# The diagonal mask of the forgetting heads on GpSimd, the output weight's pieces spread over the heads, and one output sum a step earlier

## The chip, the cores and the metric

One core of a Trainium2 chip runs the kernel. Five engines work from queues of their own: TensorE (PE; its weight loads are shown as PEld), VectorE (DVE), ScalarE (ACT), GpSimd (POOL) and SyncE (SP), which issues DMA transfers here. They meet at semaphores only. The metric is the time of one execution on the device in microseconds.

## What is computed

One step of a hybrid attention layer: a prompt of 1024 tokens and 8 running streams of 16 tokens, of width 1024. The input is normalised and projected; eight forgetting heads and eight stick-breaking heads of 64 columns attend; the group outputs are normalised, gated, and go through one output projection with a residual sum and a last norm. For the change only the prompt's forgetting heads count:

```python
def fox_attend(q, k, v, cq, ck, q_pos, k_pos):
    s = jnp.einsum("bqhd,bkhd->bhqk", q, k, preferred_element_type=jnp.float32) * (HEAD_DIM ** -0.5)
    bias = jnp.swapaxes(cq, 1, 2)[:, :, :, None] - jnp.swapaxes(ck, 1, 2)[:, :, None, :]
    mask = k_pos[None, :] <= q_pos[:, None]
    p = jax.nn.softmax(jnp.where(mask, s + bias, -jnp.inf), axis=-1)
    return jnp.einsum("bhqk,bkhd->bqhd", p.astype(v.dtype), v)
```

The queries come in 8 tiles of 128 rows. The query's own sum `cq` is constant in a row and falls out of the softmax, so the kernel adds only the key's forget sum to the scores, and masks the upper triangle of the diagonal tile.

## The kernel before, in words

The program has three stages. In the first (to about 655 us) the projection of all tokens runs beside the attention of the running streams. In the second the prompt's 16 heads follow one another, eight forgetting heads (g = 0) and then eight stick-breaking heads (g = 1). The third merges the groups and writes the output. The change is in the second stage.

**Heads and units.** A head `h` has 8 units `u`; unit `u` is query tile `i = 7 - u` and needs `8 - u` tiles of keys, so a head goes from 1024 columns down to 128. `pair` (one function on each engine) goes through the steps of two heads; `run_pairs` calls it, in a loop of the hardware for the middle pairs. Every engine's order is written out by hand, and the engines differ in which unit they hold in a step: in step `u` TensorE and VectorE work ahead on unit `u + 3` (`AHEAD`), ScalarE on unit `u + 2`. So step 5 holds the next head's unit 0, step 6 its unit 1, step 7 its unit 2.

**One unit of a forgetting head.**
- `scores` (lines 1180 to 1203, TensorE): two products for each segment of up to 512 columns, into the pair of banks of `u % 2`, then one bf16 product of `identb` and `mask[g]` that adds the mask on the diagonal tile (L1201). It waits for `s_moved` of unit u-2, which had the same banks.
- `maxima` (L1469 to L1479, VectorE): adds the forget sums `c_b` to the scores into `pr` and takes the row maximum (L1475; its second instruction reads the maximum out), then scales it (L1478). `c_b` is loaded by a DMA for each head (`load_c`), one buffer for each head of a pair, and its next load waits for the last maximum.
- `softmax` (L1373, ScalarE): the exponential with the row's sum.
- `transpose_p` (L1205, TensorE) turns the exponentials in groups of four tiles into two banks; ScalarE (even groups, L1425) and VectorE (odd groups, L1515) copy them out to `pT`.
- `outputs` (L1225, TensorE): products with the values, two units at a time, in the even steps.

**The output of a head** comes in two halves (units 0 to 3, units 4 to 7). ScalarE copies a half out (`move_o`, L1393), TensorE turns it in four transposes into bank `MI` (`turn`, L1250 to L1261), ScalarE copies its odd columns (`move_odd`, L1400), and VectorE takes the reciprocals of the row sums (L1494), adds even and odd columns (L1504) and multiplies by the reciprocals (L1506) (`store_o`, L1487). The first half is turned in step 6 (`TURN_AT`) and summed in step 7; the second half of head h-1 is turned at the end of step 4 of head h (`TURN_LAST_AT`) and copied and summed in step 5:

```python
if u == TURN_LAST_AT + 1:
    if hh:
        store_o(p, 0, 1, g)
    elif later(p, 1):
        store_o(p - 1, 1, 1, int(g and not (isinstance(p, int) and p == NPAIR)))
```

The same bank `MI` also takes the next head's keys (`turn_k_of`, L1162, in steps 1 and 2), which ScalarE rounds (`split_k`, L1370) and VectorE completes with a low part (`prep`, L1466). The turn of the second half waits for that low part (L1254).

**The output weight.** `load_wo` loads it in four parts, `split_wo` (L1615 to L1625, GpSimd) multiplies each by the norm gains in place (four instructions of 128x2048, L1621), ScalarE rounds it in eight pieces (`round_wo`, L1627, one in each step of head 6), and GpSimd writes the low parts in four instructions (L1625). In the forgetting heads GpSimd has nothing else to do. In the stick-breaking heads it has one product for each unit (L1558).

## Time and profile before

| | us |
|---|---|
| median of 3 runs (lowest, highest) | 1067.99 (1067.46, 1069.05) |
| the profiled execution's own time | 1065.78 |
| its span in the trace | 1064.0 |
| TensorE busy, share of the span | 1014.4, 95% |
| VectorE | 664.6, 62% |
| ScalarE | 463.3, 44% |
| GpSimd | 254.9, 24% |
| mean granted clock of TensorE, of full speed | 0.999 |

The profiled execution is one run, here 2.21 us below the median. Between span and time lie 1.8 us outside the first and the last instruction. Busy times overlap: an engine's share says nothing yet of what bounds a stage, and the waits in the timeline do.

### The profile page before, as it was taken

How to read it: one execution, taken by the hardware profiler on the slowest of the kernel's cores; microseconds unless marked ns; L12 is line 12 of the kernel's file. 1: busy time of each engine (PE TensorE's matmuls, PEld its weight loads, DVE VectorE, ACT ScalarE, POOL GpSimd, SP SyncE). 2: the span in 40 equal slices, each digit the busy share in tenths (PEclk: the TensorE clock that was granted, in tenths of full speed). 3: DMA queues.
4: the chain of work that ended last, by engine and by line, in shares of the span. 5: the costliest groups of instructions: out<-in, count | busy, mean ns of one | idle time of the engine just before them, and what ended most of it. 6: DMA issues, size and time to landing. Idle time of an engine off the chain costs nothing.

```text
span 1064.0 us, 27363 instructions
## 1 busy us (share of the span) xinstructions
PE 1014.4 (95%) x11316; PEld 854.3 (80%) x11316; DVE 664.6 (62%) x982; ACT 463.3 (44%) x912; POOL 254.9 (24%) x197
## 2 busy tenths in 40 slices
PE   5899999999999999999999998999988999999997
PEld 5898778986778888988888987777766788787786
DVE  5657455654665446665555723676767877787387
ACT  5522312222131232232222323676687787787453
POOL 2300000000000000111201110400065566565497
PEclk9999999999999999999999999999999999999999
DMA  6367697698889787779888787855444342421343
GB/s 228 110 238 235 226 329 294 252 363 318 305 326 339 296 304 284 301 286 362 305 314 318 278 240 238 221 138 130 112 95 98 93 110 60 99 70 51 139 159 139
DMA packets 121472, 234.02 MB, mean 220 GB/s; under 512 B 60552, under 2 KB 91272, under 8 KB 103952
## 3 DMA queue, kind: packets, MB, share of 16 engines
q1 hardware_dynamic: 96016, 209.33, 58.2%
q10 hardware_dynamic: 25344, 23.08, 6.3%
q8 instruction: 85, 1.39, 0.5%
q14 instruction: 27, 0.22, 0.1%
HBM read 204.52 MB, written 27.86 MB: 218 GB/s over the span
## 4 chain that ended last, share of the span: by engine, by line
PE 79%; DVE 6%; issue 4%; POOL 4%; ACT 4%; DMA 1%; ACTq 1%; DVEq 0%; POOLq 0%; SPq 0%
PE bank L887 29%; PE bank L874 8%; PE bank L951 7%; PE bank L997 6%; PE bank L1245 5%; PE bank L1677 5%; PE bank L1221 5%; PE bank L1198 4%; PE bank L980 3%; DVE pr L1475 2%; PE bank L1260 1%; PE bank L1176 1%; DVE om L1485 1%; POOL o_nat L1850 1%; POOL m_stat L1837 1%
## 5 line engine op out<-in xcount | busy, mean ns | idle before, releaser
L887 PE MATMUL bank<-w_hi,hT_hi 128*128 128x256 f32 (+1 forms) x896 | 261.0, 291 | 3.7 <-DVE hT_lo L620 3.3
L887 PE MATMUL bank<-w_lo,hT_hi 128*128 128x256 f32 (+1 forms) x896 | 253.4, 283 | 0.0
L887 PE MATMUL bank<-w_hi,hT_lo 128*128 128x256 f32 (+1 forms) x896 | 253.0, 282 | 0.0
L887 PEld LDWEIGHTS bank<-w_hi,hT_hi 128*128 128x128 f32 x896 | 170.9, 191 | 11.1 <-issue 5.3
L887 PEld LDWEIGHTS bank<-w_lo,hT_hi 128*128 128x128 f32 x896 | 171.1, 191 | 0.3 <-issue 0.2
L887 PEld LDWEIGHTS bank<-w_hi,hT_lo 128*128 128x128 f32 x896 | 170.7, 191 | 0.0
L534 ACT ACTIVATE u_out<-bank 128x256 f32<-128x256 f32 x112 | 42.9, 383 | 269.5 <-PE bank L887 269.2
L730 DVE STREAM_TRANSPOSE k_buf<-k_buf 128x2048 f32<-128x2048 f32 x64 | 145.3, 2292 | 3.6 <-DMA k_buf<-in_cache_sb_k 3.3
L1485 DVE TENSOR_TENSOR_SCAN om<-om 128x1024 f32<-128x1024 f32 (+3 forms) x64 | 110.4, 1729 | 14.3 <-ACT om L1386 13.6
L1558 POOL TENSOR_TENSOR pr<-pr,om 128x1023 f32<-128x1023 f32 (+3 forms) x64 | 90.4, 1419 | 77.9 <-DVE om L1485 75.1
L1221 PE MATMUL bank<-ident,pr 128*128 128x128 f32 x576 | 85.8, 276 | 8.1 <-ACT pT L1425 3.9
L1198 PE MATMUL bank<-k_hl,q_hh 128*128 128x512 f32 x192 | 76.4, 398 | 9.5 <-DVE rowmax L1475 6.0
L1245 PE MATMUL bank<-pT,v_nat 128*64 128x128 f32 x1152 | 83.6, 278 | 0.0
L747 DVE TENSOR_TENSOR_SCAN d_om<-d_om 128x2064 f32<-128x2064 f32 x8 | 35.7, 4458 | 74.6 <-ACT d_om L565 74.6
L1245 PEld LDWEIGHTS bank<-pT,v_nat 128*64 128x64 f32 x1152 | 68.1, 137 | 10.7 <-issue 10.6
L951 PE MATMUL bank<-k_buf,q_cur 32*32 32x512 f32 x2048 | 73.8, 598 | 0.4 <-issue 0.3
L1515 DVE COPY pT<-bank 128x512 f32<-128x512 f32 (+2 forms) x80 | 38.1, 476 | 55.4 <-PE bank L1221 53.1
L1221 PEld LDWEIGHTS bank<-ident,pr 128*128 128x128 f32 x576 | 61.9, 141 | 12.0 <-POOL pr L1558 3.8
L845 POOL TENSOR_TENSOR d_pn<-d_pn,d_om 128x15 f32<-128x15 f32 x8 | 3.7, 459 | 270.0 <-DVE d_om L747 270.0
L838 POOL CAST pick_cur<-pickf 128x128 fp32r<-128x128 bf16 x8 | 2.3, 293 | 272.4 <-PE bank L964 272.4
L997 PE MATMUL bank<-v_ring,d_pT 128*32 128x128 f32 x2048 | 65.9, 275 | 0.0
L1198 PE MATMUL bank<-k_hl,q_ll 128*128 128x512 f32 x192 | 64.0, 346 | 0.0
(208 smaller groups left out, 1934.2 us busy)
## 6 DMA issues: line engine op xcount, KB each, us to landing
k_buf<-in_cache_fox_k SPq DMA_DIRECT2D x32, 1024.0 KB, 9.1
v_ring<-in_cache_fox_v SPq DMA_DIRECT2D x32, 1024.0 KB, 6.8
k_buf<-in_cache_sb_k SPq DMA_DIRECT2D x32, 1024.0 KB, 8.5
v_ring<-in_cache_sb_v SPq DMA_DIRECT2D x32, 1024.0 KB, 7.1
w_raw<-in_w_in SPq DMA_DIRECT2D x14, 1024.0 KB, 9.9
out<-u_out ACTq DMA_DIRECT2D x72, 128.0 KB, 4.8
q_scratch<-u_out ACTq DMA_DIRECT2D x64, 128.0 KB, 5.3
k_nat<-out SPq DMA_DIRECT2D x32, 256.0 KB, 4.0
```

Of the source, the lines that this page charges most:

```text
L534: act.activation(u_out[:, r % UO, :], bank[:, U + i % 2, 0:NCOL], ACT.Copy).then_inc(u_moved, 1)
L730: dve.transpose(chunk, chunk).then_inc(kx_done, 1)
L874: mm = pe.matmul(bank[:, b, :], a[c % 2][:, k, cols], h[:, k, toks], start=(k == 0 and n == 0), stop=(k == KD - 1 and n == 2))
L887: mm = pe.matmul(bank[:, U + i % 2, w_cols(c)], a[:, k, hcols(s)], b[c % 2][:, k, w_cols(c)], start=(k == 0 and n == 0), stop=(k == KD - 1 ...
L951: mm = pe.matmul(bank[32 * j:32 * j + 32, DSC + r, :], q_t[rows_r, half, h, :], k_buf[rows_r, :, at:at + 32], start=(g == 1 and hh == 0 an ...
L997: mm = pe.matmul(bank[2 * DS * j:2 * DS * j + 2 * DS, MIX, 0:P], d_pT[:, 4 * c + t, 2 * DS * j:2 * DS * j + 2 * DS], v_ring[:, q % NV, t, ...
L1198: mm = pe.matmul(out, a[:, hh, i * P:i * P + P], k_hl[:, hh, seg * 512:seg * 512 + w], start=(a is q_hh), stop=(a is q_ll and not diagonal ...
L1221: mm = pe.transpose(bank[:, turn_at(u, lr, g), (j % 4) * P:(j % 4) * P + P], pr[:, u % 4, j * P:j * P + P], ident[:])
L1245: mm = pe.matmul(bank[part, PV, (i % 4) * P:(i % 4) * P + P], v_nat[:, j, hh * HD:hh * HD + HD], turned_p(hh, lr)[:, (j % 4) * P:(j % 4) * ...
L1485: dve.tensor_tensor_scan(x, x, x, 1.0, ALU.mult, ALU.bypass).then_inc(scan_done, 1)
L1558: pool.tensor_tensor(x, x, om[:, u % 4, 1:n], ALU.mult).then_inc(pb_ready, 1)
L1677: mm = pe.matmul(out, a[:, k, :], b[:, first + k, cols], start=(k == 0 and n == 0), stop=(k == NPAIR - 1 and n == 2))
```

## The change

Three things are done in the forgetting heads; the stick-breaking heads keep their order and their mask products.
- The mask product goes for g = 0. In its place GpSimd writes the masked value into the forget sums `c_b` themselves, on the 128x128 tile of unit u's diagonal (`hide_ahead`), before VectorE adds them. Earlier units of the head still need that tile unmasked, so the mask of unit u waits for `s_moved` of unit u-1 (unit 0 for the load alone), and the maximum of unit u waits for the mask (`c_hidden`).
- The pieces of the output weight become 16 multiplications and 16 low parts of 128x512. They are issued one by one behind the masks: the multiplications one in each unit of heads 1 and 2, the low parts one or two in each unit from head 6, unit 4 on.
- The second half of the last head's output is turned in step 4 before the step's transposes (before: after its outputs), its odd columns are copied in step 4 behind ScalarE's exponential, and VectorE sums it in step 4 behind the maximum, in place of step 5.

```diff
@@ scores
-                    diagonal = seg == i // 4
+                    diagonal = seg == i // 4 and g
...
-                        mm = pe.matmul(out[:, w - P:w], identb[:], mask[g][:], start=False, stop=True,
+                        mm = pe.matmul(out[:, w - P:w], identb[:], mask[1][:], start=False, stop=True,
@@ pair of TensorE
+                    if not g and u == TURN_LAST_AT and later(h, 1):
+                        turn(h - 1, 1)
                     transpose_p(p, hh, u, g)
...
-                    if u == TURN_LAST_AT and later(h, 1):
+                    if g and u == TURN_LAST_AT:
                         turn(h - 1, 1, last=following is None)
@@ pair of ScalarE
-                    if u == TURN_LAST_AT + 1 and later(h, 1):
+                    if g and u == TURN_LAST_AT + 1:
                         move_odd(h - 1, 1)
...
                         softmax(*ahead_of(p, hh, u, AHEAD - 1))
+                    if not g and u == TURN_LAST_AT and later(h, 1):
+                        move_odd(h - 1, 1)
@@ maxima
                 wait_unit_free(dve, p, hh, u)
+                dve.wait_ge(c_hidden, k + 1)
                 plain_wait(dve, sc_ready, k + 1)
@@ pair of VectorE (store_last holds the old four lines)
-                    if u == TURN_LAST_AT + 1:
+                    if g and u == TURN_LAST_AT + 1:
+                        store_last(p, hh, g)
...
                     if ahead:
                         (scans if g_ahead else maxima)(*ahead)
+                    if not g and u == TURN_LAST_AT:
+                        store_last(p, hh, g)
@@ pool_prompt
-            split_wo(pool)
+            for h in range(NHEAD // 2):
+                for u in range(NU):
+                    hide_ahead(pool, h, u)
+                    j = NU * h + u
+                    if 0 <= j - SPLIT_AT < 2 * KD:
+                        scale_wo(pool, j - SPLIT_AT)
+                    if j >= LOWS_AT:
+                        for n in range(3 * (j - LOWS_AT) // 2, min(3 * (j - LOWS_AT + 1) // 2, 2 * KD)):
+                            lower_wo(pool, n)
...
+        SPLIT_AT, LOWS_AT = NU, NU * (NHEAD // 2 - 2) + 4
+
+        def hide_ahead(pool, h, u):
+            hh, i = h % 2, TP - 1 - u
+            if u == 0:
+                pool.wait_ge(cb_loaded[hh], 16 * (h // 2 + 1))
+            else:
+                pool.wait_ge(s_moved, NU * h + u)
+            x = c_b[:, hh, i * P:i * P + P]
+            pool.affine_select(out=x, in_=x, compare_op=ALU.is_ge, fill=MASKED, base=0,
+                               pattern=[[-1, P]], channel_multiplier=1).then_inc(c_hidden, 1)
+
+        def wo_piece(ap, j):
+            return ap[:, j // 2, W * (j % 2):W * (j % 2) + W]
+
+        def scale_wo(pool, j):
+            if j == 0:
+                pool.wait_ge(gn_loaded, 32)
+            if j % 4 == 0:
+                pool.wait_ge(wr_loaded[j // 4], 16)
+            gain = gn_col[:, j // 2:j // 2 + 1].to_broadcast([P, W])
+            pool.tensor_tensor(wo_piece(wo_raw, j), wo_piece(wo_raw, j), gain, ALU.mult).then_inc(wog_done, 1)
+
+        def lower_wo(pool, j):
+            pool.wait_ge(wohi_done, j // 2 + 1)
+            pool.tensor_tensor(wo_piece(wo_lo, j), wo_piece(wo_raw, j), wo_piece(wo_hi, j).bitcast(F32), ALU.subtract
+                               ).then_inc(wolo_done, 1)
```

`round_wo` now waits for two of the smaller multiplications, and the first users of the low parts for 8 and 16 of them.

## Rows read from the trace of the kernel before

**Rows 1.** Busy time by stretch, one head each; columns in the first line.

```profile
core 0: us, PE busy (x) PEld busy (x) DVE busy (x) ACT busy (x) POOL busy (x), PEclk, DMA share, GB/s
...
709.42:727.49 18.07, 17.02 (x163) 13.73 (x159) 13.15 (x39) 12.23 (x28) 0.00 (x0) 1.00 0.49 118
...
764.45:784.64 20.19, 17.59 (x164) 13.89 (x159) 13.73 (x39) 17.27 (x34) 9.35 (x3) 1.00 0.62 138
```

**Rows 2.** Waits of TensorE, 658 to 800 us: total, times, longest.

```profile
PE bank L1198 <- DVE rowmax L1475: 6.0, 15, 0.9
```

**Rows 3.** Timeline of TensorE in head 2, steps 5 to 1: start, length, instruction.

```profile
706.04 0.48 PE L1198 MATMUL bank<-k_hl,q_hh 128*128 128x512 f32 x1
...
707.05 0.23 PE L1201 MATMUL bank<-mask_fox,identb 128*128 128x128 bf16 x1
...
707.12 0.50 PE L1221 MATMUL bank<-ident,pr 128*128 128x128 f32 x3
...
709.68 0.66 PE L1260 MATMUL bank<-ident,oT 128*128 128x128 f32 x4
...
710.71 0.50 PE L1198 MATMUL bank<-k_hl,q_hh 128*128 128x512 f32 x1 [0.36 <-DVE rowmax L1475]
...
714.57 0.19 PEld L1198 LDWEIGHTS bank<-k_hl,q_hh 128*128 128x128 f32 x1 [0.32 <-DVE rowmax L1475]
```

**Rows 4.** Timeline of head 0, steps 5 to 7, VectorE and TensorE.

```profile
672.28 0.56 DVE L1515 COPY pT<-bank 128x384 f32<-128x384 f32 x1 [2.37 <-PE bank L1221]
...
672.76 1.22 DVE L1475 CUSTOM_DVE_ANT_0 pr<-bank,c_b 128x1024 f32<-128x1024 f32 x1
...
674.31 0.66 PE L1260 MATMUL bank<-ident,oT 128*128 128x128 f32 x4
...
674.72 0.48 PE L1198 MATMUL bank<-k_hl,q_hh 128*128 128x512 f32 x1
```

**Rows 5.** Timeline of VectorE in head 2, steps 5 to 0.

```profile
707.75 0.56 DVE L1515 COPY pT<-bank 128x384 f32<-128x384 f32 x1 [2.81 <-PE bank L1221]
...
709.03 0.42 DVE L1506 TENSOR_TENSOR o_nat<-o_nat,rowinv 128x256 f32 x1
709.42 1.23 DVE L1475 CUSTOM_DVE_ANT_0 pr<-bank,c_b 128x1024 f32<-128x1024 f32 x1
...
710.89 1.09 DVE L1475 CUSTOM_DVE_ANT_0 pr<-bank,c_b 128x896 f32<-128x896 f32 x1
...
712.21 0.29 DVE L1515 COPY pT<-bank 128x128 f32<-128x128 f32 x1
...
713.56 0.95 DVE L1475 CUSTOM_DVE_ANT_0 pr<-bank,c_b 128x768 f32<-128x768 f32 x1
...
715.35 0.81 DVE L1475 CUSTOM_DVE_ANT_0 pr<-bank,c_b 128x640 f32<-128x640 f32 x1
```

**Rows 6.** Timeline of GpSimd at the start of the span.

```profile
1.23 0.29 POOL L2057 TENSOR_SCALAR_AFFINE_SELECT ident<-ident 128x128 f32<-128x128 f32 x1 [0.25 <-POOL neghalf L2055]
```

**Rows 7.** Timeline of TensorE in head 1, scores of units 0 and 4.

```profile
688.37 0.48 PE L1198 MATMUL bank<-k_hl,q_hh 128*128 128x512 f32 x1
...
696.44 0.50 PE L1198 MATMUL bank<-k_hl,q_hh 128*128 128x512 f32 x1
```

**Rows 8.** Timeline of head 3, steps 2 to 4.

```profile
719.48 0.66 PE L1176 MATMUL bank<-ident,k_nat 128*128 128x128 f32 x4
...
720.80 0.69 DVE L1466 TENSOR_TENSOR k_hl<-bank,k_hl 64x512 fp32r<-64x512 f32 x1 [0.61 <-ACT k_hl L1370]
...
721.66 0.66 PE L1221 MATMUL bank<-ident,pr 128*128 128x128 f32 x4 [0.41 <-ACT pT L1425]
```

**Rows 9.** Timeline of GpSimd and VectorE in head 0; the low parts, grouped by form.

```profile
663.35 14.28 POOL L1621 TENSOR_TENSOR wo_raw<-wo_raw,gn_col 128x2048 f32<-128x2048 f32 x4 [34.79 <-DMA wo_raw<-in_w_out]
...
676.76 1.15 DVE L1506 TENSOR_TENSOR o_nat<-o_nat,rowinv 128x256 f32<-128x256 f32 x1
...
L1625 POOL TENSOR_TENSOR wo_lo<-wo_raw,wo_hi 128x2048 fp32r<-128x2048 f32 x4 | 18.5, 4627 | 99.2 <-ACT wo_hi L1629 99.2
```

**Rows 10.** Timeline of ScalarE at the end of head 7.

```profile
800.40 0.38 ACT L1400 ACTIVATE o_odd<-bank 128x256 f32<-128x256 f32 x1 [0.96 <-PE bank L1260]
```

More of the change, by code:

```diff
@@ L1506, in store_o, with store_last @@
                     dve.tensor_tensor(dst, dst, inv, ALU.mult).then_inc(on_done, 1)
+            def store_last(p, hh, g):
+                if hh:
+                    store_o(p, 0, 1, g)
+                elif later(p, 1):
+                    store_o(p - 1, 1, 1, int(g and not (isinstance(p, int) and p == NPAIR)))
             def pair(p, g, g_next):
@@ L1515, in pair @@
                             dve.tensor_copy(*move_pt(dve, p, hh, u, n, g)).then_inc(pt_moved_dve, 1)
-                    if u == TURN_LAST_AT + 1:
-                        if hh:
-                            store_o(p, 0, 1, g)
-                        elif later(p, 1):
-                            store_o(p - 1, 1, 1, int(g and not (isinstance(p, int) and p == NPAIR)))
+                    if g and u == TURN_LAST_AT + 1:
+                        store_last(p, hh, g)
                     if u == (TURN_AT if g else TURN_AT + 1):
@@ L1613, in load_wo @@
                 sp.dma_start(wo_raw[:, 2 * c:2 * c + 2, :], wo_v[:, 2 * c:2 * c + 2, :]).then_inc(wr_loaded[c], 16)
[L1615 to L1625 removed]
+        SPLIT_AT, LOWS_AT = NU, NU * (NHEAD // 2 - 2) + 4
[21 more added lines that the diff above has]
+                               ).then_inc(wolo_done, 1)
         def round_wo(act, k):
[L1628 removed]
+            act.wait_ge(wog_done, 2 * k + 2)
             act.activation(wo_hi[:, k, :], wo_raw[:, k, :], ACT.Copy).then_inc(wohi_done, 1)
@@ L1684, in a_product @@
                 pe.wait_ge(yalo_done, s + 1)
-                pe.wait_ge(wolo_done, 2)
+                pe.wait_ge(wolo_done, KD)
             else:
```

15 lines of the change are left out of this document (2 added, 13 removed).

## The prediction

> **What bounds the kernel now.** I read the page first: TensorE is busy 95% of the span, and the lines of the change all run in one stage, the eight forgetting heads, from about 655 to 801 us. So I cut that stage at each head's first maximum. A plain head takes 18.07 us, of which TensorE is busy 17.02, VectorE 13.15 and ScalarE 12.23, with GpSimd idle [rows 1]. Head 6 takes 20.19 with ScalarE busy 17.27 (it rounds the output weight there) [rows 1]. TensorE is the bound of the head, but not everywhere: in the waits of TensorE over the stage the largest named one is the scores that wait for VectorE's maxima, 6.0 us in 15 waits [rows 2]. Then I read where in a head this wait lies, from the timeline of head 2.
>
> TensorE scores three units ahead, into two pairs of banks, so the scores of unit u wait until VectorE has reduced unit u-2. In step 5 it starts unit 0 of the next head at 706.04, turns the head's first output half at 709.68, and starts unit 2 only at 710.71, 1.03 us later [rows 3]. In head 0, where step 5 has no sum of an earlier head, the same pair stands 0.41 us apart (674.31, 674.72) [rows 4]. So 0.62 us of a head are lost there, and the timeline of VectorE says why: its copy of step 5 starts at 707.75, and the maximum of unit 0 only at 709.42 [rows 5], 1.67 us later, because reciprocal, sum and product of the previous head's second half stand between; in head 0 the maximum stands at 672.76, directly behind the copy. Everything behind is shifted too: the maximum of unit 1 at 710.89, the copy of step 7 at 712.21 [rows 5], and the scores of unit 4 at 714.57 [rows 3].
>
> **The moved sum, first stretch (unit 0 to unit 4 of the next head).** Before it takes 714.57 - 706.04 = 8.53 us [rows 3]. After the change I rebuild it from VectorE's rows. The copy starts at 707.75 less the one mask product in front of it, 707.69. From copy to maximum head 0 has 672.76 - 672.28 = 0.48 us [rows 4], so unit 0's maximum starts at 708.17 and ends 1.23 later, at 709.40. Before, the next maximum starts 710.89 - 709.42 - 1.23 = 0.24 us behind it [rows 5]. Now a GpSimd instruction lies between: the end of unit 0 releases the mask of unit 1, which releases VectorE.
>
> That round trip is shown by no row of before. The instruction itself is: an affine select of 128x128 f32 takes 0.29 us, and it started 0.25 us after the GpSimd result that it waited for [rows 6]. The lower bound is 0.29 (hand-overs free), the upper 0.25 + 0.29 + 0.25 = 0.79 (that wait on both sides). I take 0.5, since VectorE starts 0.24 us after its own result with a small instruction in between, so its own side of the hand-over must be short. Unit 1 then starts at 709.9 and ends 1.09 later, at 711.0, and the copy of step 7 starts 0.23 behind that as before, at 711.25. From that copy to unit 4's scores is 714.57 - 712.21 = 2.36 us (copy, reciprocal, sum, product, maximum of unit 2) [rows 3, 5]. The scores of unit 4 start at 713.61, 7.57 us behind 706.04: **0.96 us less**. TensorE alone would need 8.53 less the waits of 0.62 and 0.32 in it [rows 3], 7.59 with four masks or 7.33 without them, so VectorE's chain stays the bound by a little, and only one of the four removed masks counts here; the other three are worth nothing, covered by that chain. Heads 2 to 5 get this, 3.8 us. In head 1 the stretch was only 696.44 - 688.37 = 8.07 us [rows 7], so 0.5. In head 6 ScalarE is nearly full; between nothing and 1.5 I take 0.9, as its stretch is the same code with more to wait for. Sum 5.2 us.
>
> **The sum in step 4.** It isn't free of cost on TensorE: the four turns now stand in front of the step's transposes, and they wait for the second half of the next head's keys. Before, these are turned at 719.48, their low part is written at 720.80 to 721.49, the step's transposes start at 721.66 after waiting 0.41 us for ScalarE, and the turns come last, behind the outputs [rows 8]. After: the turns at about 721.6, the transposes 0.41 later at 722.05, where they no longer wait, the outputs behind them, and the next head's scores at 724.1 where they were before. So neither gain nor loss, except that the masks of units 6 and 7 lie in front of a wait and give nothing. ScalarE copies the odd columns behind its transposed copy and exponential of that step, at an estimated 724.2, so VectorE's sum and product end at about 725.4. The copy of step 5 follows the next scores by 707.75 - 706.04 = 1.71 us, so at 725.8, and before it VectorE idled 2.81 us [rows 3, 5]: that idle time hides the sum. If it ends later than 725.8, the old stall comes back by as much; the room is about 0.4 us.
>
> **The mask product.** What follows it starts 0.07 us after it (707.05, 707.12) [rows 3], and in front of it no gap is left that it alone would make. So it costs about 0.065 us; 64 would be 4.2 us. On the path are those of units 4 and 5 in the second stretch, and a 0.05 us rest: 0.18 us in each of 7 heads, 1.3 us. By the Trainium skill (TensorE: Matmul & The Clock Gate, Back-to-back issue gap) a stream of 128-column products goes at about 81 ns each; by that figure the 64 would be worth 5.2 us, and the sum would be 0.3 us larger.
>
> **The weight's pieces.** Before, GpSimd scales in four instructions from 663.35 on, 14.28 us, and VectorE's product of two SBUF inputs that started at 676.76 took 1.15 us: it ended at 677.91, 0.28 us after GpSimd's 677.63 [rows 9]; in head 2 it takes 0.42 [rows 5]. That hold of 0.7 us stands in front of unit 2's maximum and goes, as head 0 has no pieces any more: 0.75 us with a mask. A scaling piece is a sixteenth, 0.9 us, in heads 1 and 2; a lower piece is a quarter of 4.63, 1.16 us [rows 9], in heads 6 and 7, at most two in a step of 2.3 us. A mask behind a piece waits for it, but a piece starts just behind a mask, beside the maximum that this mask released. I found one late place, unit 4 of head 7 by about 0.9 us, whose scores have over 2 us of room. What such pieces can still hold is the product in step 7 of heads 1, 2 and 6: 0.1 us each, 0.3 in all, a loss.
>
> **The rest.** The first head starts cold: masks of units 1 and 2 wait on the maxima before, 2 x (0.5 - 0.24) = 0.5 us lost, TensorE waiting. At the end of head 7 ScalarE's copy of 0.38 us at 800.40 [rows 10] leaves the path to the first sigmoid: 0.4 us won. No DMA is moved; the forget sums of the next pair are loaded after the last maximum, as before.
>
> **Sum:** 5.2 + 1.3 + 0.75 + 0.4 - 0.5 - 0.3 = 6.85 us. The profiled execution took 1065.78 us (span 1064.0 and 1.8 around it), so 1058.9 for it; it was 2.2 below the median of 1067.99. Against that median, by which it will be measured: **1061.1 us**. About 2.1 us (0.2%) is what can be told from no change.
>
> **Rivals.** *A smaller gain.* The hand-over takes 0.79 and the moved turns push step 4's transposes: 6 stretches and the start's two masks lose 0.29 each (2.3 us), the rest of the second stretch 0.2 in 7 heads (1.4). Left: about 3.1, 1064.9 us. For it: every step of the new chain is serial. Against: the masks are outside the loop except at unit 1. *No change:* TensorE's turns in step 4 wait long for the keys' low part and VectorE's sum ends well behind 725.8, so the stall of step 5 stays; only hold and masks are won: 1 us, 1067.0. Against it the 2.81 us of idle time; for it that the turns' wait ends only 0.1 us ahead of where they are wanted. *Slower:* the round trip over GpSimd. Its place is between two maxima; units 0 to 1 have 0.24 us before, units 2 to 3 have 715.35 - 713.56 - 0.95 = 0.84 [rows 5]. If the trip takes 1.5 us, the first stretch loses 1.0 more, which is its gain, and unit 5's scores come 0.6 later in 7 heads (4.2), and the start loses 2.5: with what is won elsewhere some 5 us over, 1073. It decides from a trip of about 1.2 us. Such a trip needs GpSimd held by VectorE. The maximum of 1024 columns at 672.76 ran while GpSimd scaled, and took 1.22 us, as in head 2 without GpSimd (1.23) [rows 4, 5, 9], so GpSimd doesn't hold the maximum, and a maximum that isn't held is unlikely to hold GpSimd; only the product of two SBUF inputs is held. The Trainium skill (GPSIMD Engine Reference, Specifications) says that GpSimd's SBUF interfaces are shared with VectorE, with contention for VectorE instructions of two SBUF inputs or in a two-port mode; the traces agree for the first, and the maximum has one input in PSUM. *More:* the masks count everywhere and head 6 gives 1.5: 10 us, 1058.
>
> **Chances.** Forecast 0.52, smaller gain 0.20, no change 0.14, slower 0.10, more 0.04. Faster by over 0.2%: 0.76; within: 0.14; slower: 0.10. The range goes from 1057.5 (the largest case) to 1066.5, which takes in the bound 0.79 and leaves out the slower case and half of no change.
>
> **What would show it.** Plain heads of about 17.0 us; turn to unit 2's scores 0.41 us apart; maximum of unit 0 0.5 us behind the copy of step 5; maximum of unit 1 about 0.5 us behind the end of unit 0's; affine selects of 0.29 us; copies of wide tiles unchanged; the product of two SBUF inputs never over 1.5 us. It is wrong if affine selects take over 0.6 us, if VectorE idles for GpSimd in more than two units of a head, or if the sum of step 4 reaches past the copy of step 5.

## The result, and the profile after

The changed kernel took 1062.02 us (median of 4 runs, 1060.02 to 1063.22), the kernel before beside it 1068.52 (4 runs, 1067.46 to 1069.33): ratio 0.9942, 95% interval 0.9919 to 0.9965. It is faster, by 6.5 us. Two more measurements of the unchanged file are below: their medians lie 4.0 and 5.9 us under the kernel before (ratios 0.9959 and 0.9953), so this first one is the largest of three.

The profiled execution took 1063.22 us. The page of the changed kernel, first lines and the busy times:

```profile
span 1061.4 us, 27412 instructions
## 1 busy us (share of the span) xinstructions
PE 1013.3 (95%) x11252; PEld 858.1 (81%) x11252; DVE 664.3 (63%) x982; ACT 464.9 (44%) x912; POOL 277.5 (26%) x285
```

That execution is only 2.56 us shorter than the profiled one of before, and the page can't say why. Cut at the heads' first maxima, as for [rows 1], it can be said. The first maximum starts at 660.25 us, in the trace of before at 657.35: 2.9 us were lost ahead of the changed stage. The stage itself, up to the first scan (VectorE's first instruction for the stick-breaking heads), takes 140.50 us in place of 146.67, so 6.17 less; and 0.70 us come back behind it. That is a sum: the first head behind the stage alone is 1.30 us longer (last section). I compare stages from here on, because they repeat: the same kernel gave 140.50, 140.50 and 140.52 us in three traces, while its whole runs scatter by 3 to 8 us.

Busy time by stretch in the changed kernel, heads 0 to 7 and the first head behind the stage; columns as in [rows 1]:

```profile
660.25:675.83 15.58, 13.58 (x120) 11.41 (x119) 10.91 (x32) 10.83 (x24) 3.32 (x9) 1.00 0.98 326
675.83:692.75 16.92, 16.20 (x152) 13.73 (x151) 13.34 (x40) 12.35 (x28) 10.35 (x16) 1.00 0.72 177
692.75:709.94 17.19, 16.41 (x152) 13.81 (x151) 13.40 (x39) 12.36 (x28) 9.37 (x15) 1.00 0.65 151
709.94:727.29 17.35, 16.53 (x154) 13.88 (x152) 13.17 (x39) 12.36 (x28) 2.31 (x8) 1.00 0.53 126
727.29:744.76 17.47, 16.10 (x149) 13.58 (x149) 13.16 (x38) 12.38 (x28) 2.31 (x8) 1.00 0.64 150
744.76:761.88 17.12, 16.30 (x153) 13.80 (x152) 13.17 (x39) 12.35 (x28) 2.31 (x8) 1.00 0.47 121
761.88:780.67 18.79, 16.28 (x151) 13.49 (x150) 13.46 (x38) 16.74 (x34) 10.35 (x15) 1.00 0.66 148
780.67:800.75 20.08, 17.93 (x171) 14.75 (x169) 14.08 (x39) 17.10 (x34) 13.89 (x17) 1.00 0.35 82
800.75:824.36 23.61, 19.96 (x155) 16.21 (x154) 18.84 (x20) 17.82 (x36) 15.63 (x11) 0.86 0.39 82
```

The second number is the length of a head. Row 709.42 of [rows 1] (18.07 us) answers to 709.94 here (17.35), row 764.45 (20.19) to 761.88 (18.79). GpSimd, idle in a plain head before, now has its eight masks there, 2.31 us. Cut so, head 7 became longer, 20.08 from 19.38, and head 0 by 0.17. Where the cut lies matters: before, head 7's first maximum stood 3.84 us behind TensorE's first scores for it (784.64 and 780.80), now 2.03 (780.67 and 778.64). From its first scores to the first scan, head 7 takes 22.11 us in place of 23.22.

How a head was rebuilt is in the timeline of the changed kernel around the start of a head (steps 4 to 7):

```profile
705.36 0.63 PE L1261 MATMUL bank<-ident,oT 128*128 128x128 f32 x4 [0.55 <-DVE k_hl L1471]
705.82 0.60 PE L1222 MATMUL bank<-ident,pr 128*128 128x128 f32 x4
...
707.81 0.50 PE L1199 MATMUL bank<-k_hl,q_hh 128*128 128x512 f32 x1
...
708.16 0.42 DVE L1510 TENSOR_TENSOR o_nat<-bank,o_odd 128x256 f32 x1 [0.76 <-ACT o_odd L1403]
...
708.62 0.42 DVE L1512 TENSOR_TENSOR o_nat<-o_nat,rowinv 128x256 f32 x1
...
709.47 0.56 DVE L1527 COPY pT<-bank 128x384 f32<-128x384 f32 x1 [0.42 <-PE bank L1222]
...
709.94 1.21 DVE L1481 CUSTOM_DVE_ANT_0 pr<-bank,c_b 128x1024 f32<-128x1024 f32 x1
...
711.31 0.29 POOL L1643 TENSOR_SCALAR_AFFINE_SELECT c_b<-c_b 128x128 f32<-128x128 f32 x1 [3.61 <-DVE rowmax L1481]
711.31 0.42 PEld L1261 LDWEIGHTS bank<-ident,oT 128*128 128x128 f32 x4 [0.17 <-issue]
...
711.73 0.48 PE L1199 MATMUL bank<-k_hl,q_hh 128*128 128x512 f32 x1
711.77 1.09 DVE L1481 CUSTOM_DVE_ANT_0 pr<-bank,c_b 128x896 f32<-128x896 f32 x1 [0.42 <-POOL c_b L1643]
...
715.45 0.50 PE L1199 MATMUL bank<-k_hl,q_hh 128*128 128x512 f32 x1
```

The turns of the second half stand in step 4 and wait 0.55 us for the keys' low part; the step's transposes behind them wait for nothing. Sum and product end at 709.04, ahead of the copy of step 5 at 709.47, which still waits 0.42 us for TensorE: the sum is covered, with 0.43 us of room. From the copy to the maximum are 0.47 us in place of 1.67 [rows 5], and turn and next scores start 0.42 us apart in place of 1.03 [rows 3]. The maximum ends at 711.15, the affine select starts 0.16 behind it, takes 0.29, and the next maximum starts 0.17 behind that: the round trip is 0.62 us. The stretch from unit 0's scores to unit 4's is 715.45 - 707.81 = 7.64 us, in place of 8.53. A second such trip stands in every head in front of unit 7: at 706.62 its maximum starts after 0.43 us of waiting for the mask, and it starts 1.05 us behind that of unit 6, where it was 0.67 before.

Named waits in the stage, changed kernel (total, times, longest), and GpSimd's groups by form (count, then busy us and mean ns of one):

```profile
DVE pr L1481 <- POOL c_b L1643: 8.5, 18, 1.1
PE bank L1199 <- DVE rowmax L1481: 4.3, 7, 1.5
```

```profile
L1659 POOL TENSOR_TENSOR wo_lo<-wo_raw,wo_hi 128x512 fp32r<-128x512 f32 x16 | 20.3, 1283 | 0.1
L1643 POOL TENSOR_SCALAR_AFFINE_SELECT c_b<-c_b 128x128 f32<-128x128 f32 x63 | 18.6, 298 | 110.3 <-DVE rowmax L1481 110.2
L1655 POOL TENSOR_TENSOR wo_raw<-wo_raw,gn_col 128x512 f32<-128x512 f32 x16 | 16.7, 1042 | 0.0
```

TensorE waits 4.3 us for the maxima in place of 6.0 [rows 2], but its longest wait grew from 0.9 to 1.5; and there is a wait that before did not exist, of VectorE for GpSimd, 8.5 us: eight times at unit 1, eight times at unit 7, once at unit 2 (head 0) and once at unit 4 (head 7). Where the longest of both lie, the timeline of the changed kernel shows in head 7:

```profile
785.07 1.27 POOL L1659 TENSOR_TENSOR wo_lo<-wo_raw,wo_hi 128x512 fp32r<-128x512 f32 x1
...
785.22 1.40 DVE L1512 TENSOR_TENSOR o_nat<-o_nat,rowinv 128x256 f32<-128x256 f32 x1
...
787.56 0.50 PE L1199 MATMUL bank<-k_hl,q_hh 128*128 128x512 f32 x1 [1.54 <-DVE rowmax L1481]
...
787.91 2.53 POOL L1659 TENSOR_TENSOR wo_lo<-wo_raw,wo_hi 128x512 fp32r<-128x512 f32 x2
790.39 0.29 POOL L1643 TENSOR_SCALAR_AFFINE_SELECT c_b<-c_b 128x128 f32<-128x128 f32 x1
...
790.82 0.69 DVE L1481 CUSTOM_DVE_ANT_0 pr<-bank,c_b 128x512 f32<-128x512 f32 x1 [1.10 <-POOL c_b L1643]
```

The product of two SBUF inputs starts 0.15 us after a low piece of the weight and takes 1.40 us in place of 0.42; it ends at 786.62, 0.28 behind that piece's 786.34. The maximum of unit 2 follows it, and for that maximum the scores of unit 4 wait 1.54 us. And two low pieces stand on GpSimd's queue in front of the mask of unit 4, so the maximum of unit 4 waits 1.10 us.

### The profile page after: what moved, and what is told of

It reads as the page before. It is cut to its first block, busy times and chain, and to the rows that moved or that the text cites. A ratio compares the mean times of both kernels' runs of the same rounds, so it can differ in the third digit from the quotient of the medians.

```text
span 1061.4 us, 27412 instructions
## 1 busy us (share of the span) xinstructions
PE 1013.3 (95%) x11252; PEld 858.1 (81%) x11252; DVE 664.3 (63%) x982; ACT 464.9 (44%) x912; POOL 277.5 (26%) x285
## 3 DMA queue, kind: packets, MB, share of 16 engines
q8 instruction: 84, 1.38, 0.5%
## 4 chain that ended last, share of the span: by engine, by line
PE 80%; DVE 6%; POOL 5%; issue 4%; ACT 3%; DMA 1%; ACTq 1%; DVEq 0%; POOLq 0%; SPq 0%
PE bank L887 30%; PE bank L874 8%; PE bank L951 7%; PE bank L997 6%; PE bank L1246 6%; PE bank L1712 5%; PE bank L1222 5%; PE bank L1199 4%; PE bank L980 3%; DVE pr L1481 2%; PE bank L1177 1%; PE bank L1261 1%; POOL o_nat L1885 1%; POOL m_stat L1872 1%; PE bank L940 1%
## 5 line engine op out<-in xcount | busy, mean ns | idle before, releaser
L1222 PEld LDWEIGHTS bank<-ident,pr 128*128 128x128 f32 x576 | 66.0, 143 | 9.8 <-POOL pr L1577 2.4
```

What stands on the lines that cost most here:

```text
L1222: mm = pe.transpose(bank[:, turn_at(u, lr, g), (j % 4) * P:(j % 4) * P + P], pr[:, u % 4, j * P:j * P + P], ident[:])
```

## The experiments

My theory: the moved sum gives most, the masks leave TensorE for little, and the hand-over between VectorE and GpSimd takes a part back. The rivals: the masks' products on TensorE are what counted; or the affine selects cost nothing; or the weight's pieces carry the gain. Every run below was measured in five rounds beside the kernel before. The table gives, from the traces, the length of the stage and of its heads (from one maximum of 1024 columns to the next, the last to the first scan), us. The kernels are the runs below, by label; a wait that shifts a first maximum moves time from one head into the next in this table, and not out of the stage:

| kernel | stage | h0 | h1 | h2 | h3 | h4 | h5 | h6 | h7 |
|---|---|---|---|---|---|---|---|---|---|
| before | 146.67 | 15.41 | 18.71 | 17.95 | 18.07 | 18.88 | 18.08 | 20.19 | 19.38 |
| changed | 140.50 | 15.58 | 16.92 | 17.19 | 17.35 | 17.47 | 17.12 | 18.79 | 20.08 |
| sum_only | 142.07 | 15.42 | 17.11 | 17.15 | 17.21 | 17.94 | 17.22 | 20.90 | 19.12 |
| mask_on_pe | 140.28 | 15.41 | 16.96 | 17.15 | 17.22 | 17.93 | 17.22 | 18.92 | 19.47 |
| no_hide | 137.83 | 15.12 | 16.56 | 16.85 | 16.82 | 17.61 | 16.83 | 18.70 | 19.34 |
| sum_in_5 | 149.47 | 17.10 | 17.87 | 18.32 | 18.52 | 19.52 | 18.28 | 19.63 | 20.23 |
| hide_twice | 148.16 | 16.57 | 17.95 | 18.59 | 18.18 | 18.05 | 17.88 | 19.99 | 20.95 |
| mask_thrice | 149.42 | 16.24 | 18.65 | 18.41 | 18.52 | 19.22 | 18.52 | 20.19 | 19.67 |
| round_spread | 139.85 | 15.57 | 16.91 | 17.19 | 17.36 | 17.47 | 17.11 | 17.83 | 20.41 |
| two_copies | 138.58 | 15.14 | 16.60 | 16.88 | 17.18 | 17.22 | 16.95 | 18.54 | 20.07 |
| two_spread | 138.48 | 15.14 | 16.77 | 16.87 | 17.18 | 17.22 | 16.94 | 17.59 | 20.77 |
| lows_late | 137.58 | 15.14 | 16.60 | 16.88 | 17.18 | 17.22 | 16.95 | 18.54 | 19.07 |

**The change once more** (the file unchanged).

> The changed kernel unchanged. The forgetting heads, from their first maximum to the first scan behind them, took 146.7 us before and 140.5 after in the two profiles, 6.2 us less, but the projection stage before them took 2.9 us more, with a granted clock of 0.98 in one stretch of it. Theory: that 2.9 us is a chance of the one execution, so the stage of the heads again takes 140.5 +- 0.3, and the projection stage ends within 1 us of where it did before unless the clock falls again; the time is 6 to 7 us below the kernel before. Rival: the change itself delays the projection stage (code or placement), so 2 to 3 us of it come back in this profile at full clock.

Measured: 1063.64 us (12 runs, 1059.25 to 1066.95), ratio 0.9959 [0.9942, 0.9975]; stage 140.50, every head within 0.01 us of the first trace. So differences of 0.1 us in a head can be read, those of 2 us in whole runs hardly. The stage came out as expected, the rest did not: the first maximum starts at 661.02 us, 3.67 later than in the one trace of before, where under 1 us was expected, and the medians are 4.0 us apart, not 6 to 7. That fits the rival, that the change itself delays the projection stage. But over the seven other kernels that leave that stage's code as it was (those without a second copy, below) this start lies anywhere between 658.07 and 663.04, the latest in mask_thrice, which only adds products in the heads. What moves it stays open.

**The moved sum alone**, in the kernel before:

```
+  if not g and u == TURN_LAST_AT and later(h, 1):
+      turn(h - 1, 1)
   transpose_p(p, hh, u, g)
```
(and so for the odd columns, the sum and the store; masks and weight as before)

> The kernel before with the sum in step 4 alone (mask product and large pieces of the weight as before). Theory: the stall between TensorE's turn and unit 2's scores goes (0.62 us in five heads, the chain behind it too), which is most of the gain: 4 to 5 us less than before, turn to scores 0.41 us apart, and, without the mask on GpSimd, unit 1's maximum 0.24 us behind unit 0's. Rival: the masks are most of the gain, and the moved sum alone gives 2 us or less, since TensorE's saved wait comes back in front of the turns of step 4.

Measured: 1063.0 us (9 runs), ratio 0.9959 [0.9944, 0.9974]; stage 142.07, so 4.60 us less than before. That is inside the expected 4 to 5, and over the 2 us of the rival. Heads 2, 3 and 5 win 0.80, 0.86, 0.86. Head 1 wins 1.60: 0.57 because the product near its start takes 0.58 us in place of 1.15, and most of the rest because before, the first delayed maximum lay at its end, 3.10 us behind its scores (691.47, 688.37) where 2.12 is the distance now. Head 6 loses 0.71: the moved product lies in its step 4, shortly before the next head's first maximum. Its rows, of the kernel with the moved sum alone, timeline of GpSimd and VectorE:

```profile
775.95 9.30 POOL L1634 TENSOR_TENSOR wo_lo<-wo_raw,wo_hi 128x2048 fp32r<-128x2048 f32 x2 [0.59 <-ACT wo_hi L1638]
...
777.72 3.10 DVE L1510 TENSOR_TENSOR o_nat<-o_nat,rowinv 128x256 f32<-128x256 f32 x1
```

The row of GpSimd holds two instructions, the first of 4.59 us, to 780.54; the product, 0.42 us elsewhere, ends at 780.82. So the sum alone, over whole low parts, pays for this hold; the kernel before has one of 1.17 us there (783.55), in step 5.

**The sum back in step 5**, the rest as changed:

```
-  if not g and u == TURN_LAST_AT and later(h, 1):
-      turn(h - 1, 1)
...
+  if u == TURN_LAST_AT and later(h, 1):
```

> The changed kernel with the sum back in step 5 (mask on GpSimd and small pieces stay). Theory: 1 to 2.5 us less than before: one or two masks in a head count, the hold of 0.7 us in head 0 goes, and the stall of step 5 stays, made longer by the 0.37 us that a mask on GpSimd costs between two maxima. Rival, masks first: 4 us less.

Measured: 1070.26 us (12 runs), ratio 1.0019 [1.0, 1.0038]: nothing is left of the gain, and the expectation of 1 to 2.5 us fell. The stage is 149.47 us. Part of it may be the clock: the granted clock was 0.90 in head 0 and 0.91 in head 4 (but in the repeat above it was 0.94 in head 0, and that head kept its 15.58 us). Heads 2, 3 and 5, at 1.00, are 0.37, 0.45 and 0.20 us longer than in the kernel before; cut at TensorE's first scores instead, 0.34, 0.08 and 0.09. Busy time by stretch, sum_in_5, heads 2 and 3:

```profile
694.00:712.32 18.32, 16.89 (x159) 14.00 (x154) 13.39 (x39) 12.35 (x28) 9.37 (x15) 1.00 0.64 151
712.32:730.84 18.52, 16.80 (x156) 13.91 (x153) 13.16 (x40) 12.35 (x28) 2.31 (x8) 1.00 0.48 119
```

So with the sum in step 5 the masks on GpSimd win nothing and lose a little: that VectorE's chain is late already, and the round trip adds to it, is my reading. And the moved sum is worth 1.13, 1.17 and 1.16 us in these heads with the masks on GpSimd, against 0.80 to 0.86 with them on TensorE (cut at the scores: 0.91, 1.14 and 1.14 against 0.61, 0.86 and 0.85). The two parts of the change aren't additive.

**Without masks in the forgetting heads**, and **the mask's product back on TensorE**. Both start from the changed kernel and take out its affine selects with the wait on them. The first leaves the causal mask of the forgetting heads out altogether; the second puts the product back:

```
-  dve.wait_ge(c_hidden, k + 1)
...
-  pool.affine_select(out=x, in_=x, compare_op=ALU.is_ge, fill=MASKED, ...)
```
```
-  diagonal = seg == i // 4 and g
+  diagonal = seg == i // 4
...
-  mm = pe.matmul(out[:, w - P:w], identb[:], mask[1][:], ...)
+  mm = pe.matmul(out[:, w - P:w], identb[:], mask[g][:], ...)
```

> The changed kernel without the affine selects and without VectorE's wait for them; the forgetting heads then have no causal mask at all. Everything else, the pieces' places too, stays. It prices the round trip over GpSimd, which takes 0.61 us in the profile against 0.24 us between two maxima. Theory: 0.37 us in each of 7 heads and twice at the start, and the maxima that wait behind two low parts in heads 6 and 7: 2 to 4 us less than the changed kernel. Rival: VectorE's chain has room, TensorE's own work bounds the head, and the round trip is free: less than 1 us.

> The changed kernel with the mask product back on TensorE and no affine selects (sum in step 4 and small pieces stay, at the same places). Theory: near the changed kernel, within 1.5 us: what the products cost on TensorE's path (some 0.2 us in a head) about equals what the round trip costs on VectorE's; so the move of the mask is nearly worth nothing, and sum and pieces are the gain. Rival: the mask products cost their full 0.065 us each on the path, 4 us, less 2 for the round trip: 2 us slower than the changed kernel.

Measured: no_hide 1059.66 us (6 runs), ratio 0.9919 [0.9896, 0.9941], stage 137.83; mask_on_pe 1061.77 us (6 runs), ratio 0.9947 [0.9929, 0.9965], stage 140.28. Three steps can be read off. From sum_only to mask_on_pe only the weight is cut in pieces: 1.79 us less (1.98 won in head 6, where the product now takes 0.52 us, and 0.35 lost in head 7). From mask_on_pe to no_hide 64 products of 128 columns go: 2.45 us, 0.038 each. From no_hide to the changed kernel the affine selects come: 2.67 us more, 0.46 in head 0, 0.74 in head 7 and, cut at the first scores, 0.35 in heads 1 and 2 and 0.2 in each of heads 3 to 6. Both expectations held (2 to 4 us; within 1.5 us of the change). Moving the mask from TensorE to GpSimd is thus a loss of 0.2 us, all else as in the change; the gain is the sum's and the pieces'.

**Each affine select twice**, the second waiting for the first; and **each mask product three times** in the kernel before:

```
+  pool.wait_ge(c_hidden, 2 * (NU * h + u) + 1)
+  pool.affine_select(out=x, in_=x, ...).then_inc(c_hidden, 1)
...
-  dve.wait_ge(c_hidden, k + 1)
+  dve.wait_ge(c_hidden, 2 * k + 2)
```
```
+  for more in (range(0 if g else 2) if diagonal else ()):
+      pe.matmul(out[:, w - P:w], identb[:], mask[g][:], start=False, stop=False, ...)
```

> The changed kernel with every affine select issued twice, one behind the other, and VectorE waiting for the second. The round trip becomes about 1.1 to 1.2 us in place of 0.61 (0.29 us more and one more wait on GpSimd of 0.25). Theory: 0.5 us more in the stretch from unit 0 to unit 4 of each head, little elsewhere: 4 to 6 us slower than the changed kernel, so about as fast as the kernel before; that is the point where the change would turn. Rival: only where two maxima follow closely and TensorE waits for them, 2 us or less.

> The kernel before with the mask product of the forgetting heads issued three times in place of once (the masked value is three times as large, which changes no result), 128 products more. It prices one product: at 0.065 us each and all on the path, 8.3 us slower than before; with the share of masks that I took to lie on the path (3 of 8), about 3 us slower. If the added ones cost less than 1 us in all, the products are hidden and their removal gave nothing.

Measured: hide_twice 1070.57 us (12 runs), ratio 1.0028 [1.0016, 1.004], stage 148.16, 7.66 us more than the changed kernel (of it 0.99 in head 0, at a granted clock of 0.97), where 4 to 6 were expected. Timeline of hide_twice from unit 0's maximum on, which ends at 713.92:

```profile
712.70 1.22 DVE L1481 CUSTOM_DVE_ANT_0 pr<-bank,c_b 128x1024 f32<-128x1024 f32 x1
...
714.08 0.29 POOL L1643 TENSOR_SCALAR_AFFINE_SELECT c_b<-c_b 128x128 f32<-128x128 f32 x1 [2.77 <-DVE rowmax L1481]
...
714.81 0.29 POOL L1646 TENSOR_SCALAR_AFFINE_SELECT c_b<-c_b 128x128 f32<-128x128 f32 x1 [0.44 <-POOL c_b L1643]
715.34 1.09 DVE L1481 CUSTOM_DVE_ANT_0 pr<-bank,c_b 128x896 f32<-128x896 f32 x1 [1.21 <-POOL c_b L1646]
```

The trip is 715.34 - 713.92 = 1.42 us, 0.8 more than in the change (the expectation had 1.1 to 1.2 for the whole trip), and the gain is gone: this is the mechanism of the prediction's slower rival. At a trip of 1.4 the time came out on the other side of the kernel before; the prediction had it decide at about 1.2. mask_thrice took 1071.57 us (10 runs), ratio 1.0037 [1.0025, 1.005], stage 149.42: 2.75 us for 128 more products, 0.021 each, with 0.83 of it in head 0 at a granted clock of 0.96; about 3 us were expected if only some of them lie on the path.

**The roundings spread** over heads 6 and 7 (ScalarE), and the low pieces with them:

```
+  ROUND_AT = [0, 2, 4, 6, 8, 10, 11, 12]
+  LOW_AT = [4, 5, 6, 7, 8, 9, 11, 12, 12, 13, 14, 14, 15]
```

> The changed kernel with ScalarE's eight roundings of the output weight at steps 0, 2, 4, 6, 8, 10, 11 and 12 of heads 6 and 7 in place of one in each step of head 6, and GpSimd's low parts behind them one in a unit (two in two of them), none behind the mask of unit 2 of head 7, the last three behind the last mask. Head 6 took 18.8 us in the profile against 17.2 of a plain head, and TensorE waits 1.54 us in head 7 for a maximum behind a product that two low parts hold. Theory: both go, 2 to 3 us less than the changed kernel. Rival: ScalarE is as late in head 7 then, or the first product of the stick-breaking heads waits for the last low parts: no gain, or a loss of 1 us.

Measured: 1061.6 us (12 runs), ratio 0.9952 [0.9933, 0.9971]; stage 139.85. Head 6 wins 0.96, head 7 loses 0.33. The expected 2 to 3 us were missed: 0.65 came. The product of step 7 takes 0.42 us again (783.75), but the one at the end of head 7 1.25 us (796.01), beside four low pieces in a row from 794.44 on; how much of the loss is that is not shown. The whole runs don't tell it from the change.

**Two copies of the forget sums.** The measured round trip is 0.62 us where 0.24 us stood between two maxima [rows 5]. If the even units read one copy and the odd units another, the affine select of a unit waits for the maximum before last, and nothing stands between two maxima:

```
+  c_o = place(AT_H + 26624, "c_o", [P, 2, SEQ], F32)
...
-  pool.wait_ge(s_moved, NU * h + u)
+  pool.wait_ge(s_moved, NU * h + u - 1)
-  x = c_b[:, hh, i * P:i * P + P]
+  x = (c_o if u % 2 else c_b)[:, hh, i * P:i * P + P]
```
(and a transfer of its own for c_o on SP's queue, behind that for c_b)

> The changed kernel with a second copy of each head's forget sums, loaded by a transfer of its own: even units read one copy, odd units the other, so that the affine select of a unit follows the maximum before last, and the hand-over between VectorE and GpSimd (0.15 + 0.29 + 0.17 us from one maximum to the next) no longer stands between two maxima. If that hand-over is what the mask on GpSimd costs, the stage of the forgetting heads comes close to the 137.8 us that it took with no mask at all: about 138.0 (137.6 to 138.8), 2 to 2.7 us under the changed kernel's 140.5, and the run 2 to 2.7 us under it, near 1061 in this kind of measurement, ratio to the kernel before about 0.993. If it is the affine select's share of VectorE's and GpSimd's common access to memory that costs, nothing is won: 140 to 140.5. If the 512 KB more per head that the queue carries holds the next head's queries or values, heads 2, 4 and 6 become longer by over 0.3 us.

> The same with the sixteen low pieces of the output weight laid over heads 6 and 7 as in the run with the roundings spread. If the two gains are separate, the stage is 0.65 us shorter again: about 137.3 us. If the low pieces in head 7 now stand in front of masks that have slack, head 7 alone gains 0.7 us and more (20.4 to under 19.7), and the stage comes to 137.0 or below. If the pieces still hold the product of two SBUF operands on VectorE, head 7 stays above 19.9.

Measured: two_copies 1058.11 us (6 runs, 1056.77 to 1061.08), ratio 0.992 [0.9897, 0.9943]; two_spread 1060.25 us (6 runs), ratio 0.9925 [0.9902, 0.9949]. Timeline of two_copies, heads' start:

```profile
705.88 1.21 DVE L1491 CUSTOM_DVE_ANT_0 pr<-bank,c_b 128x1024 f32<-128x1024 f32 x1
...
707.25 0.29 POOL L1653 TENSOR_SCALAR_AFFINE_SELECT c_b<-c_b 128x128 f32<-128x128 f32 x1 [5.63 <-DVE rowmax L1491]
...
707.37 1.09 DVE L1491 CUSTOM_DVE_ANT_0 pr<-bank,c_o 128x896 f32<-128x896 f32 x1
```

The next maximum starts 0.28 us behind the end of the one before, without a named wait, while GpSimd masks the other copy beside it. Waits of two_copies in the stage:

```profile
DVE pr L1491 <- POOL c_o L1653: 1.6, 1, 1.6
```

18 waits of 8.5 us became one of 1.6, in front of the stage's first maximum (657.26). The stage is 138.58 us, 1.92 less than the change (2 to 2.7 were expected), 0.17 to 0.44 in each of heads 0 to 6; no head is longer, so the added transfers hold nothing. The stage of no_hide, 137.83, was not reached: in sum the rest is head 7's, 20.07 against 19.34. There the low pieces still stand. Since no maximum of head 7 waits for a mask here and the head is as long as in the change (20.08), the two late masks of the change, 1.10 and 0.86 us, cost it next to nothing. Timeline of two_copies in head 7:

```profile
779.07 2.52 POOL L1669 TENSOR_TENSOR wo_lo<-wo_raw,wo_hi 128x512 fp32r<-128x512 f32 x2
...
780.32 1.55 DVE L1522 TENSOR_TENSOR o_nat<-o_nat,rowinv 128x256 f32<-128x256 f32 x1
```

two_spread gained 0.95 in head 6 and gave back 0.70 in head 7 and 0.17 in head 1: the two gains were not separate, and the expected 137.3 was missed.

**No low piece in front of head 7's product**, on top of the two copies, and **the change beside it**:

```
+  LOWS_OF = (1, 2, 1, 2, 1, 0, 1, 1, 1, 2, 2, 2)
...
-  for n in range(3 * (j - LOWS_AT) // 2, min(3 * (j - LOWS_AT + 1) // 2, 2 * KD)):
+  for n in range(sum(LOWS_OF[:j - LOWS_AT]), sum(LOWS_OF[:j - LOWS_AT + 1])):
```

> The kernel with two copies, and the sixteen low pieces of the output weight laid so that none follows the mask of unit 1 in head 7 (1, 2, 1, 2 in head 6 from unit 4 on; 1, 0, 1, 1, 1, 2, 2, 2 in head 7). If the low pieces are what makes head 7 long (the product of two SBUF operands held for 1.55 us in place of 0.43, the mask behind it 1.6 us late), head 7 falls from 20.07 us to about 19.2 (19.0 to 19.5), and the stage from 138.6 to about 137.8; the whole run gains under 1 us on the version with two copies, which a measurement of whole runs tells hardly. If head 7 has its length from the end of step 4 and from the softmax of unit 0 that wait for other things (as in the kernel before, 19.38 us), it stays above 19.8.

> The changed kernel once more, on the same chip and in the same rounds as the kernel with two copies and late low pieces, so that the two can be set beside each other: the stage again at 140.5 us (within 0.1), the ratio to the kernel before 0.9942 to 0.996. If two copies beat the change, their ratio lies 0.002 to 0.003 below this one.

Timeline of lows_late, the same place in head 7:

```profile
778.41 0.29 POOL L1655 TENSOR_SCALAR_AFFINE_SELECT c_o<-c_o 128x128 f32<-128x128 f32 x1
781.16 0.29 POOL L1655 TENSOR_SCALAR_AFFINE_SELECT c_b<-c_b 128x128 f32<-128x128 f32 x1 [2.46 <-DVE rowmax L1491]
...
784.35 0.42 DVE L1522 TENSOR_TENSOR o_nat<-o_nat,rowinv 128x256 f32<-128x256 f32 x1
```

The product takes 0.42 us again, head 7 falls by 1.00 us to 19.07 as expected, all other heads stay as they were to 0.01 us, and the stage is 137.58 us: under that of no_hide, with the masks in. Whole runs: lows_late 1060.89 us (6 runs, 1058.98 to 1063.63), ratio 0.9931 [0.9909, 0.9953]; again_beside 1063.0 us (12 runs, 1060.67 to 1067.01), ratio 0.9953 [0.9936, 0.9971], stage 140.52. In the stage lows_late beats the change by 2.94 us, far outside what repeats differ by. In the whole runs the medians are 2.1 us apart in the expected direction, but the two intervals overlap; two_copies, measured at another time beside its own runs of the kernel before, came out lower still, though its stage is 1.0 us longer. That both beat the kernel before is measured; the order of the two, and the size against the change in whole runs, stays within the scatter.

## Why the prediction was right, and where it was not

The forecast was 6.85 us less than before. The stage gives 6.17, the medians 6.5, 4.0 and 5.9. For the profiled execution itself the prediction said 1058.9; it took 1063.22, because 2.9 us lay ahead of the stage and 1.30 in the head behind it, for which the sum has no term. That the first median met 1061.1 within 1 us is therefore partly luck; that the stage came within 0.7 us is not, as the heads show.

The prediction counts a head from TensorE's scores of its unit 0, and its "head 2" stretch begins in step 5 of head 2, so it lies in head 3. The table cuts the traces the same way, at these starts: before 670.64, 688.37, 706.04, 724.11, 742.99, 761.06, 780.80 for heads 1 to 7; changed 673.79, 690.71, 707.81, 724.82, 742.63, 759.65, 778.64. Head 0 starts at the stage's first maximum, head 7 ends at the first scan.

| | h0 | h1 | h2 | h3 | h4 | h5 | h6 | h7 |
|---|---|---|---|---|---|---|---|---|
| forecast | +0.5 | -0.93 | -0.58 | -1.04 | -1.14 | -1.14 | -1.14 | -1.38 |
| measured | +0.25 | -0.81 | -0.57 | -1.06 | -1.07 | -1.05 | -0.75 | -1.11 |

(h0: the cold start; h1: hold and masks; h2: 0.5, masks, piece; h3 to h6: stretch and masks, h3 with a piece; h7: 0.9, masks, piece, end.) Heads 2 to 5 meet the forecast within 0.09 us. Cut at the maxima, as in the table of the experiments, head 3 seems to win 0.72 and head 4 1.41: head 4's first maximum stands 2.47 us behind its scores, those of heads 3 and 5 2.13. Why, stays open; their scores start 17.01, 17.81 and 17.02 us before those of the next head.

- **The stall of step 5, and the cover in step 4: right.** Turn to scores 0.42 us (0.41 said), copy to maximum 0.47 (0.48 said), the first stretch 7.64 (7.57 said), against 8.53. From unit 4's scores to the next head's it is 9.37 (724.82 - 715.45) against 9.54, so 0.17 less (0.18 said). The turns in step 4 wait 0.55 us and the transposes behind them not at all; sum and product end 0.43 us ahead of the copy (room of 0.4 said).
- **The round trip: size too small, and one place overlooked.** 0.62 us was measured; I took 0.5 between 0.29 and 0.79. VectorE's side of the hand-over is 0.16 and 0.17 us, as argued, and not 0.25. The extra 0.12 us is more than the 0.07 by which the first stretch was missed. The prediction had masks "outside the loop except at unit 1"; the trip stands in front of unit 7 too. Over the stage, trip and masks on GpSimd cost 2.67 us (no_hide to changed), and two copies took 1.92 of it out again: that part is shown.
- **The mask product: too dear.** 0.065 us was taken from two starts in a row; taken out together, the 64 give 0.038 each, tripled, 0.021. The 5.2 us for all 64, which the prediction gave beside its own figure, were further off still: it was 2.45. But where I let only a few of a head count (0.245 us a head), 0.31 us a head came out (2.45 over 8). The price was too high and the share on the path too low, and the two nearly met: that is luck.
- **The hold by the scaling: only half of it went.** The prediction said that head 0 has no pieces any more. But in step 7 of head 0 the masks of head 1 are already being written, and the pieces stand behind them: a piece starts at 679.13, and the product at 679.70 takes 0.75 us, where it took 1.15 before. So 0.40 us were won and not 0.73. In sum_only, with the big pieces, the same product takes 0.58 us, since the stage had moved against GpSimd's start, which a transfer sets. Such a hold hangs on timing, and a term for it should have been a range.
- **The low pieces beside a product: mis-sized.** The prediction gave 0.1 us for the product in step 7 of heads 1, 2 and 6. In head 1 it took 0.75 us (696.62), in head 2 0.42 (714.09), in head 6 (785.22, so in head 7 of the tables) 1.40, which is 0.98 over the 0.42, though the row that shows how long a hold is was in front of me: a piece of 1.28 us can hold that product for a whole piece. lows_late took 1.00 us back by moving only pieces. The one late mask (unit 4, "about 0.9 us": it was 1.10) was given nothing, and two_copies bears that out.
- **Head 6: 0.39 us less than said.** From the scores of unit 5 on (771.54 before, 769.11 changed) it is 0.27 us longer than before, and 0.27 in no_hide too (768.51 to 778.04), so neither mask nor trip makes it. ScalarE is the full engine there (16.74 of 18.79 us). The cause is not shown.

The errors in heads 1, 6 and 7 (0.12, 0.39, 0.27) go one way, that of head 0 the other.

Of the rivals, "slower by the round trip" was right in mechanism, and hide_twice (slower than before at a trip of 1.42 us) agrees with a turning point between 0.62 and 1.42, where the prediction had 1.2; it was wrong for this change because the trip is short. "A smaller gain" had the trip at 0.79, which it wasn't; its 3.1 us are not far under the 4.0 of one repeat, though, and whole runs alone would not have told the two apart. "No change" wanted the sum of step 4 behind the copy; it ends 0.43 us ahead of it.

## What to carry to other kernels

Where an engine's chain is late in one step, look for the step in which it idles for another reason, and check what of the moved work then stands in front of whom: here this alone gave 4.6 us of the stage's 6.2. Before a small operation goes to an idle engine, count the hand-overs, not the operation: 0.29 us of work cost 0.62 between two dependent steps and ate what TensorE won, until a second buffer took it off the chain. And work that fills an idle engine stands in a queue: put no piece in front of an instruction that someone waits for, nor beside a VectorE product of two SBUF inputs. Before a gain or loss is put down to one round of a loop, cut the trace where the engine that sets the pace starts it: cut at VectorE's maxima, head 7 seemed to lose 0.70 us, and cut at TensorE's scores it won 1.11.

## What the runs showed of the hardware

- **A product of two SBUF inputs on VectorE is held for the whole of GpSimd's instruction, not slowed.** It ended 0.28 us behind the end of a piece at 676.76 [rows 9] and at 785.22 in head 7 (1.40 us), and as much behind a low part of 4.59 us in sum_only (3.10 us). At 780.32 in two_copies it met the seam between two pieces and was held through the second, to 781.87, 0.28 behind its end. The maximum of 1024 columns, one input in PSUM and one in SBUF, took 1.21 to 1.23 us with and without GpSimd at work. The Trainium skill (SBUF — State Buffer, SBUF: two separate sides) calls the pair of ports an exclusive lock, had for the whole instruction by whichever starts first; the traces agree, and they show the other direction too: the affine select at 779.77 in the changed kernel, beside a product that ends at 780.10, took 0.50 us in place of 0.29.
- **The two hand-overs are more than half of the trip.** 0.16 us from the end of the maximum to the affine select, 0.17 from its end to the next maximum; between two dependent affine selects on GpSimd itself 0.44 us of waiting (hide_twice).
- **The granted clock falls behind the stage in most traces, and costs time in some.** In the changed kernel the head behind the stage takes 23.61 us, with the sum alone moved 22.31, as before. Busy time by stretch of the changed kernel, then of sum_only, then of mask_on_pe:

```profile
803.75:805.75 2.00, 0.81 (x5) 0.58 (x5) 1.93 (x5) 1.47 (x3) 2.00 (x1) 1.00 0.00 0
805.75:807.75 2.00, 0.94 (x5) 0.95 (x6) 2.00 (x2) 0.69 (x2) 2.00 (x2) 0.62 0.00 0
807.75:809.75 2.00, 2.00 (x13) 1.34 (x11) 2.00 (x1) 1.91 (x5) 0.91 (x1) 0.50 0.01 4
809.75:811.75 2.00, 2.00 (x9) 1.48 (x8) 1.91 (x2) 1.41 (x3) 1.40 (x1) 0.50 0.29 68
```

```profile
803.33:805.33 2.00, 0.81 (x5) 0.58 (x5) 1.93 (x5) 1.47 (x3) 2.00 (x1) 1.00 0.00 0
805.33:807.33 2.00, 0.95 (x8) 0.85 (x8) 2.00 (x2) 0.69 (x2) 2.00 (x2) 1.00 0.00 0
```

```profile
805.35:807.35 2.00, 2.00 (x12) 1.29 (x11) 2.00 (x1) 1.91 (x5) 0.91 (x1) 0.50 0.01 4
807.35:809.35 2.00, 2.00 (x14) 1.53 (x13) 1.91 (x2) 1.93 (x5) 1.40 (x1) 0.73 0.67 152
```

In the 2 us up to 805.75 and 805.33 TensorE was equally busy (0.81 of 2.00 us) in the first two; then the granted clock went to 0.50 (1.2 in place of 2.4 GHz) in the one and stayed at 1.00 in the other. It fell to 0.50 in eleven of the fourteen traces, in all but before, sum_only and sum_in_5. Yet only in four of the eleven, the three of the changed kernel and mask_thrice's, did the head take 23.61 or 23.62 us; in the other ten traces it took 22.30 or 22.31. In those four the clock was still 0.50 in the stretch from 9 to 11 us behind the first scan (809.75 above); in the seven others it was 0.73 or more there (807.35 above). The mean clock doesn't tell it: round_spread's head had 0.85 and took 22.30 us, the changed kernel's 0.86 and 23.61. What decides when it falls stays open. Its 1.30 us stood in all three traces of the change and in none of two_copies and lows_late, and they are more than the 0.70 that came back behind the stage.
